# TensorE also sums the second tile's v rows in the three mixer stages

## What is computed

```python
def one_block(xb):                       # 128 tokens
    q = (xb @ w_q).reshape(PEER_BLOCK, PEER_HEADS, 2, PEER_HALF)
    s = jnp.einsum('thpd,hpnd->thpn', q, sub_keys).astype(jnp.float32)
    sv, si = lax.top_k(s, PEER_TOPK)
    ...                                  # 16 x 16 pairs, again the best 16
    g = jax.nn.softmax(fs, axis=-1).astype(xb.dtype)
    hid = jax.nn.gelu(jnp.einsum('td,thkd->thk', xb, u[experts]))
    return jnp.einsum('thk,thkd->td', g * hid, v[experts])
```

## Time and profile before

| | |
|---|---|
| median of 3 runs | 3902.18 us (3897.33 to 3907.54) |
| the profiled execution | 3898.55 us, span 3896.7 us |
| TensorE, DVE, ACT, POOL busy | 2408.7, 2923.2, 531.2, 2397.6 us |
| DMA | 1295.78 MB, 333 GB/s in the mean |

### The profile page before, as it was taken

One profiled execution on the slowest core, in us unless ns is written; L12 is line 12 of the kernel. 1 busy time (PEld: TensorE's weight loads), 2 busy tenths in 40 slices (PEclk: granted clock), 3 DMA queues, 4 the chain that ended last, 5 costly groups with the idle time before them and its releaser, 6 DMA issues. The chain is left out here.

```text
span 3896.7 us, 29311 instructions
## 1 busy us (share of the span) xinstructions
PE 2408.7 (62%) x8928; PEld 1667.8 (43%) x8928; DVE 2923.2 (75%) x5647; ACT 531.2 (14%) x1237; POOL 2397.6 (62%) x2052
## 2 busy tenths in 40 slices
PE   8899527786798617767598717687788815600000
PEld 6676412464585313345486413355576513200000
DVE  2311786788877896778888797788777797798889
ACT  2310001122211101112110101122210101100000
POOL 0000377776675677766676577776566577777775
PEclk9989769997798859888698958998799968955555
DMA  4234699999899889999899989999799988999998
GB/s 176 96 107 140 213 324 361 369 392 348 294 408 409 339 316 347 368 384 392 325 389 409 352 321 347 361 390 391 291 365 409 370 323 308 355 350 367 368 387 339
DMA packets 359900, 1295.78 MB, mean 333 GB/s; under 512 B 40512, under 2 KB 40768, under 8 KB 359744
## 3 DMA queue, kind: packets, MB, share of 16 engines
q0 software_dynamic: 294912, 1073.87, 72.9%
q1 hardware_dynamic: 64256, 217.94, 14.8%
q10 hardware_dynamic: 576, 2.10, 0.1%
HBM read 1291.65 MB, written 2.10 MB: 332 GB/s over the span
## 5 line engine op out<-in xcount | busy, mean ns | idle before, releaser
L1057 POOL DMA_INDIRECT ring<-in_peer_u,eidx x1024 | 1222.6, 1194 | 960.1 <-DVE eidx L1181 475.1
L1057 POOL DMA_INDIRECT ring<-in_peer_v,eidx x1024 | 1174.8, 1147 | 516.8 <-issue 288.1
L1094 DVE CUSTOM_DVE_ANT_0 ring<-ring,hp 128x1024 f32<-128x1024 f32 x1024 | 1236.4, 1224 | 266.0 <-DMA ring<-in_peer_u,eidx 254.1
L1099 DVE SCALAR_TENSOR_TENSOR acc<-ring,wgt,acc 128x1024 f32<-128x1024 f32 x744 | 949.2, 1290 | 123.4 <-DMA ring<-in_peer_v,eidx 101.2
L519 PE MATMUL bank<-xt,panel 128*128 128x256 f32 x4096 | 952.8, 392 | 33.7 <-ACT raw L854 8.5
L519 PEld LDWEIGHTS bank<-xt,panel 128*128 128x128 f32 x4096 | 804.1, 198 | 164.0 <-issue 27.0
L752 PE MATMUL bank<-ring,dg 128*128 128x512 f32 x1120 | 549.6, 632 | 497.2 <-ACT dg L826 363.7
L752 PEld LDWEIGHTS bank<-ring,dg 128*128 128x128 f32 x1120 | 208.9, 198 | 825.4 <-issue 578.6
L594 PE MATMUL bank<-dg,ex 128*128 128x128 f32 x640 | 112.8, 349 | 149.2 <-DVE dg L1341 84.5
L594 PEld LDWEIGHTS bank<-dg,ex 128*128 128x128 f32 x640 | 105.4, 257 | 161.3 <-issue 145.7
L715 PE MATMUL bank<-yt,panel 128*128 128x256 f32 x768 | 173.6, 379 | 0.0
(11 more groups left out here) (164 smaller groups left out, 1884.0 us busy)
## 6 DMA issues: line engine op xcount, KB each, us to landing
panel<-in_panels SPq DMA_DIRECT2D x368, 512.0 KB
ring<-in_peer_u,eidx POOLq DMA_INDIRECT x1024
ring<-in_peer_v,eidx POOLq DMA_INDIRECT x1024
work<-in_rel_bias SPq DMA_DIRECT2D x16, 512.0 KB
gb<-in_ln_g SPq DMA_DIRECT2D x8, 512.0 KB
gb<-in_ln_b SPq DMA_DIRECT2D x8, 512.0 KB
panel<-in_keys SPq DMA_DIRECT2D x16, 256.0 KB
work<-in_x SPq DMA_DIRECT2D x4, 512.0 KB, 5.2
```

What stands on the lines that cost most here:

```text
L1057: pool.indirect_dma_start(ring[:, n % RING, :], None, t_in["peer_u" if kind == "U" else "peer_v"], bass.IndirectOffsetOnAxis(ap=eidx[:, t, ...
L1094: v.tensor_tensor_reduce(row, row, hp[:, t, :], 1.0, 0.0, ALU.mult, ALU.add, hid[:, t, c:c + 1]).then_inc(used, 1)
L1099: stt(out=acc[:, t, :], in0=row, scalar=wgt[:, t, c:c + 1], in1=acc[:, t, :], op0=ALU.mult, op1=ALU.add).then_inc(used, 1)
```

## The change

138 more v rows go to TensorE: those of tile 1 in stages A, B and C of phases 1, 2 and 3 (19, 10 and 17 a phase). Their diagonals are written by ACT into `xd`, a part of `work` that is otherwise `xn`'s, and they accumulate in banks 6 and 7, which stay open from lane 2 of one phase until lane 0 of the next; tile 0 keeps its two groups. So that banks 6 and 7 are free in the mixers, the weighed scores have one bank (1), shared with the attention outputs; q, k and the swap share bank 0; the v projections go to banks 0 and 1 in A and 2 and 3 in C. The second q and k projection of C goes to bank 1. The 16 rows ahead of stage A are cut into four places. The wait for `add_sums` moves from ahead of the turn to ahead of A's first scores. `add_sums` adds only the banks whose group ends there: two at a phase's end, four after lane 0, and two more at the very end.

```diff
-                plan.append(((s, stage, -1, 0), before))
+                plan += [((s, stage, -1, i), k) for i, k in enumerate(spread(before, 4 if stage == "A" else 1))]
...
-    return kind == "V" and stage == "T" and (it > 1 or it == 0 and k % 2 == 1)
+    if kind == "U":
+        return False
+    return stage == "T" and (it > 1 or it == 0 and k % 2 == 1) or stage in "ABC" and t == 1
...
+def group_of(n):
+
+    t = STREAM[n % ROWS][3]
+    return (2 * (n // ROWS + 1) - 1 if t else sum_group(n)), t
...
+        xd = work[:, 14336:16384].rearrange("p (i c) -> p i c", c=P)
+
+        def sum_diag(n):
+            i = PE_PLACE[n] % DIAGS
+            return dg[:, i, :] if KEY_OF[n][1] == "T" else xd[:, i, :]
...
-        tp = bank[6:8]
+        tp = bank[1]
...
             def project_qk(kind, s, u):
...
+                b = bank[1] if kind == "C" and u == 1 else bank[0]
+                if kind == "C" and u == 1:
+                    pe.wait_ge(bg_ev, s * 2 + 1)
+                elif u:
                     pe.wait_ge(qk_ev[kind], n)
...
             def weigh(kind, s, u):
...
-                    if f < 2 and u:
-                        pe.wait_ge(pt_ev[kind], c - min(2, len(fills(s, kind))) + 1 if len(fills(s, kind)) > 1 else c)
-                    if f >= 2:
-                        pe.wait_ge(pt_ev[kind], c - 1)
+                        if kind == "C":
+                            pe.wait_ge(qk_ev["C"], n + 2)
+                    if f == 0 and u:
+                        pe.wait_ge(o_ev[kind], n)
+                    if f:
+                        pe.wait_ge(pt_ev[kind], c)
...
             def stage_a(s):
                 project_qk("A", s, 0)
+                sums((s, "A", -1, 1))
                 project_qk("A", s, 1)
+                sums((s, "A", -1, 2))
+                if s:
+                    pe.wait_ge(added, 2 * s - 1)
                 scores("A", s, 0)
-                project_v("A", s)
+                sums((s, "A", -1, 3))
+                pe.wait_ge(qk_ev["A"], s * UNITS + 2)
+                project_v("A", s, bank[0:2])
+                for i in range(4):
+                    sums((s, "A", 0, i))
                 for u in range(UNITS):
                     weigh("A", s, u)
                     if u + 1 < UNITS:
                         scores("A", s, u + 1)
+                    sums((s, "A", u, 4))
                     outputs("A", s, u)
+                    if u + 1 < UNITS:
+                        sums((s, "A", u + 1, 0))
+                        sums((s, "A", u + 1, 1))
                     if u + 2 < UNITS:
                         project_qk("A", s, u + 2)
+                    if u + 1 < UNITS:
+                        sums((s, "A", u + 1, 2))
+                        sums((s, "A", u + 1, 3))
...
             def stage_b(s):
...
+                    if j == 0:
+                        sums((s, "B", 0, 0))
                 pe.wait_ge(bd_in, 16 * (s // 2 + 1))
                 inputs_b(s, 0)
+                sums((s, "B", 0, 1))
                 pe.wait_ge(bx_ev, s * 2 + 1)
-                pe.wait_ge(bg_ev, s * 2 + 1)
                 project_qk("C", s, 0)
                 project_qk("C", s, 1)
+                sums((s, "B", 0, 2))
+                sums((s, "B", 0, 3))
                 swap_qk(s, 0)
+                sums((s, "B", 1, 0))
                 inputs_b(s, 1)
-                pe.wait_ge(pt_ev["A"], fills_before(s, "A", UNITS))
-                project_v("C", s)
-
-            def stage_c(s):
+                sums((s, "B", 1, 1))
                 pe.wait_ge(bx_ev, (s + 1) * 2)
                 pe.wait_ge(bg_ev, (s + 1) * 2)
+                project_v("C", s, bank[2:4])
+                sums((s, "B", 1, 2))
+                sums((s, "B", 1, 3))
+
+            def stage_c(s):
                 pe.wait_ge(ri_act, (s + 1) * 2)
+                pe.wait_ge(v_ev["C"], (s + 1) * TILES)
+                sums((s, "C", -1, 0))
                 scores("C", s, 0)
...
                 if s:
                     pe.wait_ge(tq_ev, s * 16)
-                    pe.wait_ge(added, 2 * s - 1)
                 turn(xn, bank[0:2], ready, x_turned, x_taken, s * 4)
...
+                sums((s, "A", -1, 0))
                 stage_a(s)
...
             def add_sums(group):
 
-                dve.wait_ge(pe_used, max(PE_PLACE[GROUP_ROWS[(group, t)][-1]] for t in range(TILES)) + 1)
+                tiles = [t for t in range(TILES) if (group, t) in GROUP_ROWS]
+                last = max(GROUP_ROWS[(group, t)][-1] for t in tiles)
+                if group % 2 == 0:
+                    last = max(last, last_in_lanes(group // 2))
+                dve.wait_ge(pe_used, PE_PLACE[last] + 1)
```

More of the change, by code:

```diff
@@ L168, in sum_group @@
     s, stage, it, i = KEY_OF[n]
-    return 2 * s + (it > 0) - 1
+    return 2 * s + (stage == "T" and it > 0) - 1
+def group_of(n):
+    t = STREAM[n % ROWS][3]
+    return (2 * (n // ROWS + 1) - 1 if t else sum_group(n)), t
 GROUP_ROWS = {}
 for _n in PE_SUMS:
-    GROUP_ROWS.setdefault((sum_group(_n), STREAM[_n % ROWS][3]), []).append(_n)
+    GROUP_ROWS.setdefault(group_of(_n), []).append(_n)
 def rows_of(key):
@@ L180, in rows_of, with last_in_lanes @@
     return range(lo, hi)
+def last_in_lanes(s):
+    return max(n for n in PE_SUMS if KEY_OF[n][:2] == (s, "T") and KEY_OF[n][2] == LANES - 1)
 class Own:
@@ L541, in project_qk, with project_v @@
                     w = weights(s, kind, qk_panel(u, j))
-                    dense(bank[0][:, j * HALF:(j + 1) * HALF], w, xt).then_inc(panel_done, 1)
-            def project_v(kind, s):
+                    dense(b[:, j * HALF:(j + 1) * HALF], w, xt).then_inc(panel_done, 1)
+            def project_v(kind, s, banks):
                 for j in range(4):
@@ L627, in swap_qk @@
                 pe.wait_ge(qk_ev["C"], n + 1)
-                if u >= 2:
-                    pe.wait_ge(o_ev["C"], n - 1)
-                mm(bank[1][:, :], swap, raw[:, u % 2].rearrange("p a t -> p (a t)"), start=True, stop=True
+                mm(bank[0][:, :], swap, raw[:, u % 2].rearrange("p a t -> p (a t)"), start=True, stop=True
                    ).then_inc(swapped, 1)
@@ L849, in take_qk @@
                     else:
-                        src = bank[0][:, j * HALF:(j + 1) * HALF]
+                        src = b[:, j * HALF:(j + 1) * HALF]
                         if j == 0:
@@ L893, in stage_a @@
                 take_qk("A", s, 0)
+                gelus((s, "A", -1, 1))
                 take_qk("A", s, 1)
+                gelus((s, "A", -1, 2))
+                gelus((s, "A", -1, 3))
                 exps("A", s, 0)
-                take_v("A", s)
+                take_v("A", s, bank[0:2])
                 for u in range(UNITS):
@@ L945, in stage_b @@
                         take_qk("C", s, 1)
+                take_v("C", s, bank[2:4])
             def stage_c(s):
@@ L964, in stage_c @@
                     o = (2 * UNITS + 2 * j) * HALF
-                    fn(yt[:, o:o + 512], tp[j][:, :], ACT.Copy, scale=subg[:, 0:1]).then_inc(yc_ev, 1)
+                    fn(yt[:, o:o + 512], bank[j][:, :], ACT.Copy, scale=subg[:, 0:1]).then_inc(yc_ev, 1)
             def stage_g(s):
@@ L1350, in attention_stage @@
                 else:
-                    rows((s, "A", -1, 0))
+                    for i in range(4):
+                        rows((s, "A", -1, i))
                 for u in range(UNITS):
```

35 lines of the change are left out of this document (22 added, 13 removed).

## The result

Measured: 4021.14 us (median of 4 runs, 4016.85 to 4032.96) against 3904.86 before, ratio 1.0295 [1.0271, 1.0319]. The profiled execution took 4016.85 us, span 4015.0. I had forecast 3915 in 3880 to 3950: the sign was right, the size was not, +118 us between the two profiles where I had +14.5. In a second group of runs (e6) it was 1.0348 [1.0318, 1.0378].

The account below looks back on a forecast made before the run. DVE was busiest (75%, TensorE 62%), but stage A of phases 1 and 3 had only 15.6 us of TensorE left. Terms 44 - 3 + 0 - 16 - 13 + 2.5 = +14.5 us gave 3913, median 3917; forecast 3915, range 3880 to 3950.

Parts of the forecast that it names:

- Price of a row: Each moved row: 1.72 us on TensorE at the full clock, at most 3.4 at the half clock; 1.20 us saved on DVE.
- The conditions of a sum: Every sum on TensorE waits for its row landed, its diagonal written and all ahead in the queue; 0.3 us more each.
- R1: Rival, slower by much: added waits are the larger part, 0.3 us for each of 138 sums, +41 us, 3957; chance 0.15.
- Stage B, 'I take 0 each': Stage B, three times: 13 sums, 22.4 us, against 24.3 us of TensorE not busy; 0 each, from -3 to +6.
- Stage A, odd phases, +22: Stage A of phases 1 and 3: sums and fills lengthen TensorE's queue, +22 us a phase, between +10 and +28.
- unit 2: A's unit without a projection, odd phases: DVE, three rows lighter, is ready earlier and the 7.53 us wait is filled; -0.3 us.
- the end: Last term of stage A's sum in phases 1 and 3, after unit 2: +0.4 us.
- Phase 2's A, forecast at -3: Stage A of phase 2: TensorE comes to 123.5 of 125.7 us; -3 us, between -8 and +6.
- The units' fills: Stage A: with one bank each fill of weighed scores waits for ACT's copy of the one before; four units, 5 to 8 us.
- Stage C, -29: Stage C with fewer rows on DVE: -8 us in each of phases 1 and 3, -13 in phase 2.
- R2: Rival, faster: filled gaps bring back TensorE's full clock in C and B, -36 us, 3866; chance 0.24 together with smaller gains.
- Phase 0, +2.5: Phase 0, no rows but the single bank: fills 4 x 0.57, v copy wait 1.2, one 1 us wait gone; +2.5 us.

Follow-up runs that it names:

- e6: The changed kernel, unchanged, run again in a second group beside the variants; ratio to the kernel before 1.0348 [1.0318, 1.0378].
- e3: Changed kernel with only the 81 second-tile rows of stages B and C summed on TensorE, A's 57 back on DVE; ratio to before 1.0115.
- e10: Changed kernel with only stage C's 51 second-tile rows on TensorE, A's and B's back on DVE; ratio to before 1.0041.
- e15: Changed kernel with only C's rows and B's three late rows a phase on TensorE (60), two banks in turn in A; ratio to before 0.9992.
- e16: Changed kernel, one bank, with the 3 rows a phase between the halves of B's first projections back on DVE; ratio to before 1.0209.
- e11: Changed kernel with 10 rows a phase back on DVE: 7 before A's first weigh, 3 between B's first projections; ratio to before 1.0137.
- e12: Layout alone, second run: changed kernel with no row sums of stages A, B and C on TensorE; ratio to before 1.0139.
- e14: Changed kernel with no row sums of A, B and C on TensorE, two banks in turn for A's weighed scores only; ratio to before 1.0007.
- prompt groups: Three groups of runs whose profiles show no ACT wait ending with a remote releaser; the kernel before took 3853 to 3870 us.
- late groups: Three groups whose profiles show some ACT waits ending with a remote releaser, starts up to 4 us late; the kernel before took 3905 to 3923 us.
- e5: The kernel before, unchanged, run once more with a profile beside the variants; 3907.6 us.
- e8: Changed kernel with only B's and C's 81 rows on TensorE and weighed scores alternating between banks 1 and 0; ratio to before 1.0150.
- e9: Changed kernel with each of the 138 sums issuing only its first half of 512 columns; ratio to before 1.0150.
- e7: Changed kernel with all its sums, weighed scores alternating between banks 1 and 0 in all stages; ratio to before 1.0300.
- e17: Changed kernel with all 138 sums, two banks in turn for stage A's weighed scores only; ratio to before 1.0245.

## Why the prediction was wrong, step by step

Of the 103.8 us between my sum and the two profiles, A has 31.5, B 30.7, C 32.2, phase 0 13.0, and the rest -3.6.

- **Price of a row**, 1.72 us on TensorE: that was the pitch at the full clock; 2.13 of busy time measured over the 138, 57 us more in all. Part of what failed.
- **The conditions of a sum** stood in R1, priced at 0.3 us each and argued away with 'DVE consumes the same rows earlier, so most have landed'. That sentence is the step that failed where the gathers are concerned. It asked whether the row is there for the sum, and not who waits for the slot that the sum holds. (About the row it was nearly right: TensorE's idle time before the 138 sums is 67.0 us, 0.49 a row where R1 had 0.3, and of it 32.9 are for the diagonal and 24.7 for the row.) I had named what is queued behind the sums on TensorE, but not what is queued behind them on GpSimd.
- **Stage B, 'I take 0 each'**: +30.7 measured. TensorE had 24 us free there, as I read in the earlier trace rows, but not at the moments at which the rows fall due. The later first tanh was priced rightly, 6.7 us: DVE's wait for it grew by 6.0, from 10.1 to 16.1. What failed is the sentence behind it, 'Later DVE has 8 rows less, 9.6 us', which was to give that back: DVE waited 17.4 us for u rows instead. e3 against e10 gives 38 us for B's rows, e15 20 us for nine of them, placed where TensorE idles; e16 against e3 gives 27 us of B for the nine early ones.
- **Stage A, odd phases, +22**: +40.7 and +25.6. Term by term, phase 1 and then 3: up to the first weigh +16.4 and +8.7 (I had +8.4); unit 0 +8.4 both times (+8.2); unit 1 +5.2 both times (+4.9); unit 2 +5.9 and +0.9 (-0.3); the end +4.7 and +2.4 (+0.4). So the first two units were right to 0.3 us here, and the head, unit 2 and the end were sized too small. By the wait rows of phase 1 the path was the one I had, TensorE's queue ahead of DVE's scores, with 17.6 us of waiting for u rows that I didn't have. In phase 1 a late copy of ACT falls into unit 2. Phase 2's A, forecast at -3, gave +6.2. For the seven sums at the head e16 against e11 gives 28 us by the ratios and 40 by the windows, over three phases. The units' fills were 'four units 5 to 8 us'; about 10 a phase measured (e12, e14). The end was the term sized 0.4, and with one bank it is 6.5 us longer than with two (e12, e14), 1.9 of it waits and the rest half clock.
- **Stage C, -29**: where C's rows stand alone B and C are 22 us shorter than before, 30.5 shorter than the layout alone (e10). Beside the sums of A and B C's own gain is still there in prompt groups: C takes 327.9 us in e16, whose work in C is the changed kernel's, 328.8 in e3, and 355.3 in the layout alone (e12). In late groups it isn't: 350.3 and 365.6 in the changed kernel's two profiles, against 347.1 and 349.9 in before's. One unit of the first shows a late copy of ACT (below); what else loses the gain there is open.
- **R2** had the clock's direction right: with C's sums it rose from 0.66 to 0.86 in C of phase 1 (e10). The Trainium skill ('TensorE: Matmul & The Clock Gate', HAM oscillation) has idle gaps put the array back to the half clock and continuous work keep it; that agrees in direction. But R2 priced C at -48, and B and C together gave -22 to -30.5.
- **R1** was nearest in sign and size, 3957, and still 64 us short.
- **Phase 0, +2.5**: +15.5 in this pair, some 8 over all profiles; the rest is the place of the half clock in these executions (e6).
- The parts, layout 46 to 54, A 46, B 29 to 38, C -30 to -38, sum to about 95 us; the changed kernel showed 115 and 136. What makes the difference is open. The parts were measured in prompt groups and the changed kernel in late ones: its C is 22 to 38 us longer than e16's and its A, 1570.7 and 1576.3, 17 to 22 longer than e16's 1554.0. But before is itself 35 to 70 us slower in late groups and has no prompt profile, so how much of this the ratios hold isn't known. A candidate for the cause is ACT's late starts. An example after, where a fill ended at 1058.5 and its copy came at 1062.24:
```profile
1056.51 1.95 PE L618 MATMUL bank<-dg,ex 128*128 128x128 f32 x16
1062.87 2.93 PE L618 MATMUL bank<-dg,ex 128*128 128x128 f32 x12 [4.42 <-ACT work L931]
...
1062.24 0.58 ACT L931 COPY work<-bank 128x512 f32<-128x512 f32 x1 [6.52 <-remote]
```
TensorE waits for that copy and then runs at the half clock for the next 20 us; the unit takes 39.6 us in all, the same unit 32.2 in e3 and in e16. Why ACT is late in some groups only, no run shows, nor that this is all that sets the groups apart. e5 to e8 (late) and e9 to e12 (prompt) are recorded for a chip of the same number, so it may not be the chip.

## What to carry to other kernels

An instruction that takes a buffer off an in-order ring is on the path of everything that is fetched after it: before moving it to an idle engine, look at what stands ahead of it in that engine's queue and compare that time with what the ring holds. Idle time averaged over a stage is no place to put work. In C of phase 1 (e10) GpSimd stood 20.2 us at the sums' slots too, but DVE waited for no row there, and the rows were a gain; in B (e15) it stood 15.8 us, DVE waited 9.8 for u rows, and they were a loss. So the trace to read is the other consumer's wait, not TensorE's. And a bank given away has a price of its own: two banks in turn in A, and C's rows alone, turned +3.0% into -0.6%. The Trainium skill ('Perfetto Trace Analysis', Matmuls) says that independent matmul groups should rotate through banks so that the copy of one overlaps the next; e14 agrees in A, by 1.3%, and e7 against e17 shows C, where it did not help (455 us over four phases against 439 with one bank).

## What was not expected of the hardware

- Identical instructions of phase 0, eleven profiles of the one-bank layout: 393.5 to 410.2 us up to the turn of hp, and the longer the stretches at 1.2 GHz the longer the phase: 32 us of them in the shortest, 72 in the longest. A single profile can't tell 10 us there.
- With four waits of 0.6 us each between its fills TensorE ran at the half level for 13 us (e12); one long run of fills after a similar idle time (7.5 and 9.7 us) was back at full speed for the outputs (e14). From the last weigh to B's projection every odd phase without sums in A took 16.2 to 16.7 us with one bank and 9.7 to 11.0 with two in turn in A only. That the waits did it, and not the point at which the clock fell, is an inference.
- A float32 matmul of 512 columns takes 0.86 us at the full clock, in two records. The Trainium skill ('FP8 and Floating Point Precision', TensorE Precision Notes) gives four passes for true FP32; 4 x 512 columns at 2.4 GHz are 0.85 us, an estimate from that page, and the trace agrees.
